# A two-part token table, a later read of the count, and other quarters for the mod steps of layer 1

## What is computed

```
mod = silu(c) @ w_mod[l] + b_mod[l]
h = rms_norm(x, norm_ffn[l]) * (1 + sc2) + sh2
layer 0: f = (silu(h @ w1) * (h @ w3)) @ w2
layer 1: logits = h @ router_w + router_b; top 2, softmax of the two
         f = sum over e of weight[e] * swiglu(h, w1[e], w3[e], w2[e])
x = x + g2 * f
```

## Time and profile before

| | us |
|---|---|
| median of 3 runs | 1548.92 (1548.36 to 1551.69) |
| profiled execution | 1548.98 |
| its span, first to last instruction | 1547.3 |
| busy PE / DVE / ACT / POOL | 1517.8 / 1293.8 / 961.6 / 86.1 |

### The profile page before, as it was taken

One profiled execution on the slowest core, in us unless ns is written; L12 is line 12 of the kernel. 1 busy time (PEld: TensorE's weight loads), 2 busy tenths in 40 slices (PEclk: granted clock), 3 DMA queues, 4 the chain that ended last, 5 costly groups with the idle time before them and its releaser, 6 DMA issues.

```text
span 1547.3 us, 19088 instructions
## 1 busy us (share of the span) xinstructions
PE 1517.8 (98%) x7751; PEld 1237.7 (80%) x7751; DVE 1293.8 (84%) x1168; ACT 961.6 (62%) x835; POOL 86.1 (6%) x139
## 2 busy tenths in 40 slices
PE   8999999999999989999999999999999999999997
PEld 4885789999888558888888888888888888888885
DVE  5888888888774579989899998888998988998996
ACT  3532434444544347777777777787777787777775
POOL 5300100000000020100000000000010000000000
PEclk9999999999999989999999999999999999999999
DMA  9776788887824169999999999999999999999990
GB/s 347 280 266 224 245 322 325 305 297 273 313 68 151 55 249 353 369 389 386 364 357 391 358 398 388 368 350 383 370 391 379 374 356 372 383 365 371 411 371 30
DMA packets 161460, 493.08 MB, mean 319 GB/s; under 512 B 4570, under 2 KB 8838, under 8 KB 161366
## 3 DMA queue, kind: packets, MB, share of 16 engines
q1 hardware_dynamic: 156160, 475.02, 82.1%
q0 software_dynamic: 4384, 14.59, 2.5%
q10 hardware_dynamic: 822, 2.18, 0.4%
HBM read 483.91 MB, written 7.86 MB: 318 GB/s over the span
## 4 chain that ended last, share of the span: by engine, by line
PE 92%; DVE 4%; DMA 1%; SPq 1%; ACT 1%; issue 0%; POOL 0%; ACTq 0%; DVEq 0%
PE bank L1275 20%; PE bank L1276 20%; PE bank L1277 20%; PE bank L950 6%; PE bank L1135 4%; PE bank L947 3%; PE bank L1174 3%; PE bank L1176 3%; PE bank L1175 3%; PE bank L1150 2%; PE bank L1151 2%; PE bank L1308 2%; PE bank L1152 2%; DMA ring<-in_w_mod_dram 1%; PE bank L866 1%; DVE ring_low L1975 1%
## 5 line engine op out<-in xcount | busy, mean ns | idle before, releaser
L1975 DVE TENSOR_TENSOR ring_low<-ring,w_high 128x2048 fp32r<-128x2048 f32 x336 | 768.1, 2292 | 97.7 <-ACT w_high L2451 91.7
L2451 ACT ACTIVATE w_high<-ring 128x2048 fp32r<-128x2048 f32 x336 | 646.2, 1925 | 231.8 <-PE bank L1277 219.5
L1275 PE MATMUL bank<-w_high,x_high 128*128 128x512 f32 x896 | 352.9, 394 | 2.1 <-DVE ring_low L1975 2.1
L1276 PE MATMUL bank<-ring_low,x_high 128*128 128x512 f32 x896 | 351.4, 392 | 0.0
L1277 PE MATMUL bank<-w_high,x_low 128*128 128x512 f32 x896 | 348.9, 389 | 0.0
L1275 PEld LDWEIGHTS bank<-w_high,x_high 128*128 128x128 f32 x896 | 168.5, 188 | 39.5 <-DVE ring_low L1975 3.4
L1277 PEld LDWEIGHTS bank<-w_high,x_low 128*128 128x128 f32 x896 | 168.2, 188 | 37.4
L1276 PEld LDWEIGHTS bank<-ring_low,x_high 128*128 128x128 f32 x896 | 168.3, 188 | 34.7
L2386 ACT ACTIVATE tmp_r<-ring 128x1024 fp32r<-128x1024 f32 x84 | 89.0, 1062 | 146.5 <-PE bank L1176 85.8
L1275 PE MATMUL bank<-w_high,act_high 128*128 128x512 f32 x448 | 178.8, 399 | 0.2 <-DVE ring_low L1975 0.2
L1276 PE MATMUL bank<-ring_low,act_high 128*128 128x512 f32 x448 | 177.7, 397 | 0.0
(11 more groups left out here) (362 smaller groups left out, 1625.3 us busy)
## 6 DMA issues: line engine op xcount, KB each, us to landing
ring<-in_moe_w_dram SPq DMA_DIRECT2D x168, 2048.0 KB, 9.1
ring<-in_w_mod_dram SPq DMA_DIRECT2D x23, 2048.0 KB, 12.9
ring<-in_ffn_w_dram SPq DMA_DIRECT2D x21, 2048.0 KB, 13.9
ring<-in_w_in_dram SPq DMA_DIRECT2D x7, 2048.0 KB, 18.5
ring<-in_w_out_dram SPq DMA_DIRECT2D x4, 2048.0 KB, 8.0
ring<-in_w_in_dram SPq DMA_DIRECT2D x4, 1024.0 KB, 15.6
ring<-in_w_mod_dram SPq DMA_DIRECT2D x2, 1024.0 KB, 15.9
gate_row<-in_b_mod_dram POOLq DMA_DIRECT2D x4, 512.0 KB, 8.8
```

Of the source, the lines that this page charges most:

```text
L1275: mm(out_, x_h, w_h, start=first, stop=False)
L1276: mm(out_, x_h, w_l, start=False, stop=False)
L1975: tt_(moe_low(u, m // 2)[:, c], moe_slot(u, m // 2)[:, c], w_high[:, m % HIGHS, :].bitcast(F32), ALU.subtract).then_inc(low_made, 1)
L2451: act(w_high[:, m % HIGHS, :], moe_slot(u, m // 2)[:, c], ACT.Copy).then_inc(high_made, 1)
```

## The change

Three edits. The table: ACT issues no DMA any more; POOL subtracts without waiting for one, then itself writes the table in one DMA from `xn_high` and adds `xn_low` to it by an accumulating DMA, with a wait between; the gathers for group 1 wait for both. The count: DVE and ACT read it after the first group of two experts, not before it. The mod steps: group 0 keeps its own in m = 0 to 7; the steps of layer 1's parts stand in quarters 4 to 11 of each group of twelve.

```diff
--- before.py
+++ after.py
@@ -402,7 +402,7 @@
         s_zero = sem("expert_rows_cleared")
         s_rows_out = sem("expert_rows_written")
         s_rows_in = sem("expert_rows_read")
-        s_tokens = [sem(f"token_rows_{tt}_written") for tt in range(TT)]
+        s_tokens = sem("token_rows_written")
         s_again = sem("token_rows_read_again")
         s_gathered = sem("token_rows_gathered")
 
@@ -801,10 +801,13 @@
             eng.wait_ge(norm_t.sem, norm_t.at("t3", 3))
             for tt in range(TT):
                 eng.wait_ge(split_a.sem, split_a.at(f"x{tt}"))
-                eng.wait_ge(s_tokens[tt], 16)
                 done(eng, eng.tensor_tensor(xn_low[:, tt, :], xn[:, tt, :], xn_high[:, tt, :].bitcast(F32),
                                             ALU.subtract).then_inc(split_v.sem, 1), split_v, f"x{tt}")
 
+            table = token_rows[:, :].rearrange("(t p) d -> p t d", p=P)
+            eng.dma_start(table, xn_high[:, :, :].bitcast(F32)).then_inc(s_tokens, 16)
+            eng.wait_ge(s_tokens, 16)
+            eng.dma_start(table, xn_low[:, :, :].bitcast(F32), accum_op=ALU.add).then_inc(s_tokens, 16)
             eng.wait_ge(gather_t.sem, gather_t.at("g3", 0))
             eng.memset(y_low.bitcast(F32), 0.0).then_inc(s_clear, 1)
             eng.wait_ge(s_clear, 1)
@@ -823,6 +826,8 @@
 
             def tokens_in(g):
 
+                if g == 1:
+                    eng.wait_ge(s_tokens, 32)
                 eng.wait_ge(index_v.sem, index_v.at("i", g))
                 eng.wait_ge(gather_t.sem, gather_t.at("g3", g - 1))
                 for u in range(PAIR):
@@ -1857,8 +1862,12 @@
                              ffn_v, f"a{i}", jj)
                     if m == 12:
                         gate(0, 1, (bank[6], bank[7]))
-                    if kind != "w2":
-                        mod_step(*((1, j - 1) if j else (0, 5)), m - QUARTER["w1", j, 0])
+                    if m < QUARTER["w1", 1, 0]:
+                        mod_step(0, 5, m)
+                    elif QUARTER["w1", 1, 0] + 4 <= m < QUARTER["w2", NJ - 1, 0]:
+                        at = m - QUARTER["w1", 1, 0]
+                        if at % 12 >= 4:
+                            mod_step(1, at // 12, at % 12 - 4)
                     if kind == "w2" and hb == 1 and 1 <= j < 5:
                         mod_columns(1, MOD_PARTS[j - 1])
                     if (kind, hb) == ("w1", 3) and j:
@@ -2119,9 +2128,10 @@
                     fill_low(part, pair(q, 0), 0)
                 if q == 0:
                     token_weights()
-                    most_tokens.append(eng.value_load(most_i[0:1, 0:1], min_val=0, max_val=T))
                     for g in range(NE // PAIR):
                         two_experts(q, g)
+                        if g == 0:
+                            most_tokens.append(eng.value_load(most_i[0:1, 0:1], min_val=0, max_val=T))
                 else:
                     with eng.Fori(0, NE // PAIR) as g:
                         two_experts(q, g)
@@ -2275,7 +2285,6 @@
             def token_high(tt):
 
                 eng.wait_ge(norm_v.sem, norm_v.at(f"xn{tt}", 3))
-                eng.dma_start(token_rows[tt * P:(tt + 1) * P, :], xn[:, tt, :]).then_inc(s_tokens[tt], 16)
                 done(eng, act(xn_high[:, tt, :], xn[:, tt, :], ACT.Copy).then_inc(split_a.sem, 1), split_a, f"x{tt}")
 
             def mixers(l):
@@ -2530,10 +2539,11 @@
                         eng.wait_ge(fill_b.sem, others)
                     fill_high(part, pair(q, 0), 0, lambda: eng.wait_ge(fill_b.sem, others))
                 if q == 0:
-                    eng.wait_ge(route_v.sem, route_v.at("most_i"))
-                    most_tokens.append(eng.value_load(most_i[0:1, 0:1], min_val=0, max_val=T))
                     for g in range(NE // PAIR):
                         two_experts(q, g)
+                        if g == 0:
+                            eng.wait_ge(route_v.sem, route_v.at("most_i"))
+                            most_tokens.append(eng.value_load(most_i[0:1, 0:1], min_val=0, max_val=T))
                 else:
                     with eng.Fori(0, NE // PAIR) as g:
                         two_experts(q, g)
```

## The result

The changed kernel takes 1539.83 us (median of 4 runs, 1539.76 to 1540.99) against 1550.08 us of the kernel before (4 runs, 1548.36 to 1551.69): ratio 0.9941, 95% interval 0.9926 to 0.9956, so 0.4 to 0.7% faster. Run again (changed_again) it takes 1538.69 us (6 runs) against 1548.17 us (13 runs on the same chip): 0.9933 (0.9918 to 0.9947). The forecast was 1541.8 us, with a range of 1537.0 to 1545.5, and 7.2 us less than the kernel before; the medians differ by 10.25 us.

The account below looks back on a forecast made before the run. PE is busy 98% of the span, so only its idle or lower-clock stretches can give time. C -3.1, A -1.9 and B -2.2 sum to -7.2 us, from 1548.98 to 1541.8 us; range 1537.0 to 1545.5.

Parts of the forecast that it names:

- Part C: Dense FFN, layer 1's mod steps moved to quarters 4 to 11: two PE stalls go, -3.6 + 0.5 = -3.1 us.
- The ring's shift: FFN weight loads: mod chunks released four quarters later, delaying a w2 load some 4 us; costed at nothing, otherwise 1 to 4.
- the last group was the weak place: FFN group 6: extras of 3.8 us against a lead of 3.1; 0.5 us of new stall, bounds 0 and 3.6.
- Part A: Routing, token table: POOL's waits for the table's DMA go, gather at 560.5 for 562.38, -1.9 us, bounds 0 and -4.1.
- rival 2: Routing: POOL's subtractions block DVE as long as before, only elsewhere; Part A gives 0, 1543.7 us; chance 0.15.
- if the clock still falls: Routing: condition under which PE's counts and keep-clock pass let the gather begin at 560.5 for 562.38, -1.9 us.
- rival 1: Routing and gather: the clock stays up as PE's idle before the counts shrinks; 3.2 us more, 1538.6 us; chance 0.24.
- The norm products: Routing: four DVE products beside POOL's first subtraction go free; cost 0, bounds 0 and 2 us.
- The accumulating write: POOL's added 1 MB DMA to the table, before group 1's gathers: takes 10 to 18 us, cost 0, bounds 0 and 8.
- Rival 4: Accumulating DMA is slow, clears queue behind it, DVE waits at first act low parts; 1558 us at 35 us; chance 0.03.
- Part B: After the gather, count read later: PE's stall at unit 3 of expert 0 goes, -2.2 us, bounds -2.2 and -1.2.
- The sum: Whole kernel: C -3.1, A -1.9, B -2.2 give -7.2 us, 1541.8 us; chance 0.44.

Follow-up runs that it names:

- split_low: Changed kernel with DVE's low part of unit 2 cut in two halves and the last FFN group's mod steps back in quarters 0 to 7: 1538.28 us, 0.9930.
- a_only: The kernel before with the two-part token table alone: 1546.15 us, ratio 0.9985.
- b_only: The kernel before with the later count alone: 1547.25 us, ratio 0.9991.
- before_keep5: The kernel before with 5 instead of 3 idle-time passes of PE ahead of the router's counts: 1550.27 us, ratio 1.0007.
- own_place: The kernel before, exact table kept, with xn's low part in its own place so POOL needs no wait for the table's DMA: 1545.43 us, 0.9980.
- a_and_c: The changed kernel without the later count (count read where it was): 1543.32 us, ratio 0.9962.
- no_subtraction: The kernel before with POOL's two subtractions replaced by memsets, the tokens' low part left out of the gather: 1546.13 us, ratio 0.9980.
- split_keep4: split_low with 4 instead of 3 idle-time passes of PE ahead of the counts: 1537.39 us, ratio 0.9922.

## Why the prediction was right, step by step

- **Part C.** Forecast -3.1 us: the two stalls of the FFN out, 0.5 of new stall in. The stalls went, the new one is 0.65 us, the stage is 2.8 to 3.3 us shorter; at the same clock it is 2.4. The forecast was right, perhaps a little large. The ring's shift, costed at nothing, shows nowhere as a wait. That the last group was the weak place is borne out: with its steps in the first eight quarters the wait goes (split_low).
- **Part A, the mechanism.** The first subtraction at 547.26 (forecast 547.24), norm products not stretched (rival 2 falls), one held instruction in the chain and none at `dispatch`: as said. Two sizes were forecast too long: the second subtraction ended at 553.96, not 554.4, so the counts came at 556.12, not 556.6; and from counts to gather I took 3.9 us, where the profile has 2.7 (a_only too, with the clock down in part of it).
- **Part A, the clock.** The step that failed is "if the clock still falls". I took the fall of the kernel before over whole (557 to 568) for a start 1.9 us sooner. It is gone in the changed kernel, in both profiles, and shorter in the three kernels that have A without B. What I gave 0.24 as rival 1 (3.2 us more, 1538.6) is the nearer to what happened: the medians are 1539.8 and 1538.7, and the difference to before is 10.25 us where I forecast 7.2. That the forecast time is only 2.0 us off is in part luck, for the kernel before was 1.2 us slower in these runs than in those I started from. The reason that rival 1 gives, shorter idle before the counts, is not the whole of it. There were two idles, the second before the gather (2.37 us in b_only, 0.46 now), and before_keep5 shows that the fall comes with the second too, when the first is down to 0.51. And the fall came without long idle in a_only, own_place, a_and_c and split_low. What is shown is that the runs of the changed kernel have a higher mean clock (0.996 for 0.993); why the routing keeps its clock in one execution and not in the next stays open.
- **The norm products.** The four norm products take 2.28 us from 546.85 on, beside POOL's subtraction from 547.26, and 2.28 us in the kernel before, with none beside them: they are not held. In no_subtraction POOL's memset at 558.55 lies beside short instructions of 0.17 to 0.18 us, some with two SBUF inputs, and none is held. By the Trainium skill (SBUF — State Buffer, § Who interferes with whom) a DVE instruction with one SBUF input and outside a two-port mode is not held by a reading GpSimd instruction, and a GpSimd instruction that only writes holds none with two. These traces agree with both.
- **The table's DMAs.** The accumulating write landed in 8.5 us, where I had put 10 to 18; DVE's first activation low part, at 601.34, shows no wait for the clear. Rival 4 falls. The traffic added is 1 MB (494.12 MB for 493.08), not the 2 MB that I reckoned with, since the table was written before too.
- **Part B.** The forecast was -2.2; measured are 2.3 to 2.8 us, by the stage and at the same clock. A term that I missed lies between A and B: in all three kernels with A and without B the stall at unit 3 is followed by a fall of the clock (1.7 us in a_only), and B takes the stall out. In the four kernels with the stall and without A no fall follows it; why is not shown.
- **The sum.** The forecast was -7.2, with the clock as before. At the same clock the three alone give -2.4 - 1.6 - 2.6 = -6.6, and the whole -6.1 and -6.7: they add up. If each is taken against before on its own chip, it is -5.8 for the three and -7.1 for the whole, so that they add up is shown only to about a us. Beside it stand 3.4 to 4.1 us by the clock, of which A alone has 1.3 and A with C 2.1. The rest, 1.3 to 2.0, is about the size of the one fall at unit 3 (1.7).

## What to carry to other kernels

Where PE passes through thin work, list every idle of it in that stretch, not the largest alone: in before_keep5 one idle was filled and the fall of the clock came at the next. And take more than one profile before you put a fall down to an edit. When an instruction is held and a DMA wait stands just behind it, price both; removing the first alone wins only their difference. Compare stages between common points of the two traces before adding up an edit: 3.2 us of unrelated clock in layer 0's mixers would have hidden all of part C here.

## What was not expected of the hardware

- The kernel before runs from 1546.6 to 1556.2 us, and nearly nine tenths of the variance go with the mean granted clock. In layer 0's mixers, where all kernels do the same, the falls at 101 and 127 are there in some profiles and not in others; so the clock differs between executions of the same work. The fall at 102.8 in the changed kernel came while PE was busy without a break (20.00 of 20 us from 90 to 110), and so did that of split_keep4 at 504.8 (15.00 of 15 us from 490 to 505).
- A fall lasts into busy work: in the kernel before the clock was down until 567.5 though PE had been busy from 562.4 on (the gather and the first matmuls of expert 0).
- The hold goes both ways within 6 us: DVE's low part waited 0.3 us for POOL (2.60 for 2.29), POOL then 1.4 us for DVE (3.75 for 2.34), and DVE's next 0.8 us for POOL.
